# A trunk of token mixers on one core: inverse of both directions in lockstep, pair 0 prepared one stage earlier, gram products in four groups, two products per chunk in the recurrence

## What is computed

```python
def _rwkv_direction(r, w, k, v, a, b, s0):
    def step(state, inp):
        r_t, w_t, k_t, v_t, a_t, b_t = inp
        sa = jnp.einsum('bhvk,bhk->bhv', state, a_t)
        state = (state * w_t[:, :, None, :] + sa[..., None] * b_t[:, :, None, :]
                 + v_t[..., None] * k_t[:, :, None, :])
        return state, jnp.einsum('bhvk,bhk->bhv', state, r_t)
...
    kk = heads(k * lp['rw_k_k'])
    kk = kk * lax.rsqrt(jnp.maximum(jnp.sum(kk * kk, axis=-1, keepdims=True), 1e-24))
    k = k * (1.0 + (a - 1.0) * lp['rw_k_a'])
...
    a_vec, b_vec = -kk, kk * a
    o_f, s_f = _rwkv_direction(r, decay[:, :, 0], k, v, a_vec, b_vec, s0[:, 0])
    o_b, s_b = _rwkv_direction(_flip(r), _flip(decay[:, :, 1]), _flip(k), _flip(v),
                               _flip(a_vec), _flip(b_vec), s0[:, 1])
    o = o_f + _flip(o_b)
```

## Time and profile before

| | us |
|---|---|
| median of three runs (1967.83 to 1978.81) | 1972.71 |
| the profiled execution, its own time | 1975.78 |
| span of that execution | 1974.0 |
| PE busy | 1885.5 (96%) |
| DVE busy | 1092.9 (55%) |
| ACT busy | 744.2 (38%) |
| POOL busy | 32.1 (2%) |
| mixers stage, layer 0 (470.5 to 700.8) | 230.3 |
| mixers stage, layer 1 (1427.3 to 1649.1) | 221.8 |

### The profile page before, as it was taken

The page is one execution under the profiler, slowest core; times in us unless marked ns, Lnnn a source line. Parts: engine busy times, 40 slices in busy tenths (PEclk is TensorE's granted clock), DMA queues, the critical chain, the costliest instruction groups (busy, mean ns, idle before and its releaser), DMA issues. The chain is left out here.

```text
span 1974.0 us, 38649 instructions
## 1 busy us (share of the span) xinstructions
PE 1885.5 (96%) x16410; PEld 1739.0 (88%) x16410; DVE 1092.9 (55%) x1853; ACT 744.2 (38%) x1117; POOL 32.1 (2%) x64
## 2 busy tenths in 40 slices
PE   5999999998889999999999999999978899999998
PEld 3988999996666789999999999999947688999997
DVE  3544444865766475555455554477576746655533
ACT  3333333345334254333343333344363324433322
POOL 0000000000001000000000000000000100000000
PEclk9999999998999999999999999999989999999999
DMA  7766233423446343332343333342241412333332
GB/s 280 275 221 220 103 119 136 176 86 93 129 152 219 115 147 128 127 123 100 132 147 128 127 116 108 127 187 95 78 131 49 130 50 87 128 117 119 106 132 91
DMA packets 73335, 263.25 MB, mean 133 GB/s; under 512 B 9712, under 2 KB 11120, under 8 KB 57072
## 3 DMA queue, kind: packets, MB, share of 16 engines
q1 hardware_dynamic: 73200, 261.27, 39.0%
HBM read 259.08 MB, written 2.16 MB: 132 GB/s over the span
## 5 line engine op out<-in xcount | busy, mean ns | idle before, releaser
L160 PE MATMUL ps<-h_head,w_head 128*128 128x386 f32 x1824 | 623.5, 342 | 4.1 <-ACT h_head L293 2.1
L160 PE MATMUL ps<-h_head,w_rest 128*128 128x386 f32 x1824 | 619.3, 340 | 0.0
L160 PE MATMUL ps<-h_rest,w_head 128*128 128x386 f32 x1824 | 617.3, 339 | 0.0
L223 ACT ACTIVATE w_head<-w_raw 128x2048 fp32r<-128x2048 f32 (+1 forms) x176 | 303.0, 1722 | 606.0 <-PE ps L160 588.8
L226 DVE TENSOR_TENSOR w_rest<-w_raw,w_head 128x2048 fp32r<-128x2048 f32 (+1 forms) x176 | 360.6, 2049 | 209.3 <-ACT w_head L223 209.3
L160 PEld LDWEIGHTS ps<-h_head,w_head 128*128 128x128 f32 x1824 | 345.8, 190 | 23.1 <-issue 16.9
L160 PEld LDWEIGHTS ps<-h_head,w_rest 128*128 128x128 f32 x1824 | 345.9, 190 | 0.0
L160 PEld LDWEIGHTS ps<-h_rest,w_head 128*128 128x128 f32 x1824 | 343.0, 188 | 0.2
L160 PE MATMUL ps<-gu_head,w_head 128*128 128x384 f32 x832 | 278.4, 335 | 0.1
L160 PE MATMUL ps<-gu_head,w_rest 128*128 128x384 f32 x832 | 277.7, 334 | 0.0
L160 PE MATMUL ps<-gu_rest,w_head 128*128 128x384 f32 x832 | 277.7, 334 | 0.0
(11 more groups left out here) (300 smaller groups left out, 1784.2 us busy)
## 6 DMA issues: line engine op xcount, KB each, us to landing
w_raw<-in_w_in SPq DMA_DIRECT2D x88, 1024.0 KB, 4.8
w_raw<-in_w_out SPq DMA_DIRECT2D x64, 704.0 KB, 4.1
w_raw<-in_ada_w SPq DMA_DIRECT2D x41, 1024.0 KB, 6.3
ada_raw<-in_ada_w SPq DMA_DIRECT2D x31, 1024.0 KB, 6.3
w_raw<-in_mix_in SPq DMA_DIRECT2D x26, 1024.0 KB, 4.8
w_raw<-in_mix_out SPq DMA_DIRECT2D x8, 1024.0 KB, 5.0
hyena_const<-in_hconst SPq DMA_DIRECT2D x2, 1792.0 KB, 9.4
x<-in_x_in SPq DMA_DIRECT2D x1, 1536.0 KB, 12.1
```

Source lines behind the costliest of these rows:

```text
L160: return nc.tensor.matmul(out, lhsT, rhs, start=start, stop=stop)
L223: return nc.scalar.activation(self.HI[src], self.RAW[src], ACT.Copy)
```

## The change

Four parts, all in `mix_in_stage`, `mixers_stage` and `Pair`.

1. **Lockstep.** `each` goes through both directions inside each chunk and head, so that four products on the four 64x64 quadrants follow each other. Direction 1 reads or writes the other half of the partitions (`near`, `far`); its additions on DVE and GpSimd become two instructions of 64 partitions each.
2. **Gram.** Four groups (direction, three chunks) of 64x128 on two banks, and the turned keys as products of their own against a constant identity (`pe_turn_keys`), copied out by ACT from a third bank. The identity that GpSimd wrote is gone.
3. **Recurrence.** New `pe_values_in` (gram of the keys with the values), `pe_turn_a` and `pe_solve_a` (inverse with a), all ahead of the recurrence; its step is then `pe_y` and `pe_u`, without the copy to `XS`.
4. **Places.** Pair 0's low-rank products, norm, scans, exponentials and unit keys go into units n = 10 to 12 of `mix_in_stage`; pairs B and C are prepared together while A is in its recurrence (C with bank 6 alone); one `Ada` of two slots carries all sets. Each engine has a list for layer 0 (four sets) and another for layer 1 (two).

```diff
-            def each(self, b, lhsT, rhs):
-                for c, e in PROBS:
-                    last = mm(bank(b, TOK)[half(e), c * C:c * C + C], lhsT(c, e), rhs(c, e))
-                return last
+            def each(self, banks, lhsT, rhs, name, to):
+                for c in range(NCH):
+                    for e in range(2):
+                        for z in range(2):
+                            last = mm(bank(banks[z], TOK)[half(to[z] ^ e), c * C:c * C + C], lhsT(z, c, e), rhs(z, c, e))
...
+            def near(self, z, e):
+                return half(e)
+            def far(self, z, e):
+                return half(e ^ z)
...
-            def pe_s2(self, pe, z):
-                ba, _ = self.pair_banks(z)
-                self.after_act(pe, f"s1_{z}")
-                self.after_dve(pe, f"s1_{z}")
-                self.pe_step(self.each(ba, self.power(z), self.of(self.D2, z)), f"s2_{z}")
+            def pe_s2(self, pe):
+                self.both(pe, self.after_act, "s1")
+                self.both(pe, self.after_dve, "s1")
+                self.each(self.first_banks(), self.power(self.far), self.of(self.D2, self.far), "s2", (0, 0))
...
+            def side(self, z, first, second, name):
+                for c in range(NCH):
                     for e in range(2):
-                        at = (self.b0 + ((3 * z + b) * 2 + e) % 3) * 512 + k * 192
-                        last = mm(PS[:, at:at + 192], self.BK[half(e), z, 2 * b + k, :, :].rearrange("p x t -> p (x t)"),
-                                  self.AR[half(e), z, b, 2 * k:2 * k + 3, :].rearrange("p x t -> p (x t)"))
-                self.pe_step(last, f"gram{z}{b}")
+                        last = mm(bank(self.b1, TOK)[half(e), c * C:c * C + C], first(z, c, e), second(z, c, e))
+                self.pe_step(last, f"{name}_{z}")
...
+            def pe_turn_keys(self, pe, z, e):
...
+                    self.after_act(pe, f"bt{(2 * z + e - 1) // 2}{(2 * z + e - 1) % 2}")
+                for c in range(NCH):
+                    last = mm(bank(self.b2, TOK)[:, c * C:c * C + C], self.BK[half(e), z, c, :, :].rearrange("p x t -> p (x t)"),
+                              cst("istack", 0, None, 64 * e, 64 * e + 64))
...
+            def pe_solve_a(self, pe):
+                self.both(pe, self.after_dve, "s9")
+                self.both(pe, self.after_act, "at")
+                self.each(self.first_banks(), lambda z, c, e: self.MR[half(e), z, c, 1, 0:C], self.of(self.Y, self.near), "w", (0, 0))
...
             def dve_y(self, dve, i, z):
                 ba, _ = self.pair_banks(z)
                 self.after_pe(dve, f"s{i}_{z}")
-                self.tt(self.Y[:, z, :, :], self.XQ[:, z, :, 1, :], bank(ba, TOK).rearrange("p (c t) -> p c t", t=C), ALU.add, f"s{i}_{z}")
+                product = bank(ba, TOK).rearrange("p (c t) -> p c t", t=C)
+                if z == 0:
+                    last = nc.vector.tensor_tensor(self.Y[:, 0, :, :], self.XQ[:, 0, :, 1, :], product, ALU.add)
+                else:
+                    for e in range(2):
+                        last = nc.vector.tensor_tensor(self.Y[half(e), 1, :, :], self.QB[half(e)], product[half(1 - e)], ALU.add)
+                self.dve_step(last, f"s{i}_{z}")
...
+                        if n == 10:
+                            A.act_key_rate(act)
+                            A.act_key_factor(act)
+                            A.act_decays(act)
+                            A.act_key_root(act)
...
-                B.shared_free, C.shared_free = (A.act_done, A.AC["s6_1"]), (B.act_done, B.AC["s6_1"])
-                half = sets // 2
-                C_RAW = Place(B_AT.at)
-                ADAS = (Ada(None, SEMS[10:15], 2, [7] * half, 1, None, mod_row),
-                        Ada(C_RAW, SEMS[26:32], 3, [7] * half, 1, None, PR[:, 0:2 * NP - 2:NP, 0:ADA_W // 2].unsqueeze(1)))
+                B.shared_free, C.shared_free = (C.dve_done, C.DV["kk"]), (B.act_done, B.AC["s6_1"])
+                ADA = Ada(None, SEMS[10:15], 2, [7] * sets, 1, None, mod_row)
```

More of the change, by code:

```diff
@@ new lines, in each, with both @@
+            def each(self, banks, lhsT, rhs, name, to):
[3 more added lines that the diff above has]
+                            last = mm(bank(banks[z], TOK)[half(to[z] ^ e), c * C:c * C + C], lhsT(z, c, e), rhs(z, c, e))
+                            if name and (c, e) == (NCH - 1, 1):
+                                self.pe_step(last, f"{name}_{z}")
+            def both(self, pe, after, *names):
+                for name in names:
+                    for z in range(2):
+                        after(pe, f"{name}{z}" if name == "q" else f"{name}_{z}")
@@ L1738, in pe_spread_v @@
                 self.after_dve(pe, "vinv")
[L1739 to L1745 removed]
+                self.pe_step(spread_heads(self.b2, self.NRV), "vspread")
             def pool_decay(self, pool):
@@ L1940, in dve_power_q @@
                     nc.vector.tensor_copy(xq[:, :, :, 0, :], products[:, :, :, 0, :])
-                    last = nc.vector.tensor_tensor(xq[:, :, :, 1, :], xq[:, :, :, 1, :], products[:, :, :, 1, :], ALU.add)
+                    if z == 0:
+                        last = nc.vector.tensor_tensor(xq[:, :, :, 1, :], xq[:, :, :, 1, :], products[:, :, :, 1, :], ALU.add)
+                    else:
+                        q1 = self.QB[:, first:first + 3 * n, :].rearrange("p (b c) t -> p b c t", b=n)
+                        for e in range(2):
+                            last = nc.vector.tensor_tensor(q1[half(e)], xq[half(1 - e), :, :, 1, :], products[half(e), :, :, 1, :], ALU.add)
                 self.dve_step(last, f"s2q_{z}")
@@ L1946, in dve_q @@
                 self.after_pe(dve, f"s{i}_{z}")
-                self.tt(self.XQ[:, z, :, 1, :], self.XQ[:, z, :, 1, :], bank(bb, TOK).rearrange("p (c t) -> p c t", t=C), ALU.add, f"s{i}_{z}")
+                product = bank(bb, TOK).rearrange("p (c t) -> p c t", t=C)
+                if z == 0:
+                    last = nc.vector.tensor_tensor(self.XQ[:, 0, :, 1, :], self.XQ[:, 0, :, 1, :], product, ALU.add)
+                else:
+                    old, new = (self.QB, self.XQ[:, 1, :, 1, :]) if i == "3q" else (self.XQ[:, 1, :, 1, :], self.QB)
+                    for e in range(2):
+                        last = nc.vector.tensor_tensor(new[half(e)], old[half(1 - e)], product[half(e)], ALU.add)
+                self.dve_step(last, f"s{i}_{z}")
             def dve_y(self, dve, i, z):
@@ new lines, in mixers_stage @@
+                assert homes.ceiling <= nc.sbuf_top and LEFT.at <= homes.early_at and RIGHT.at <= late_at
+                B_ROWS, B_LEFT, B_RIGHT = Place(homes.rows_at), Place(homes.above), Place(homes.right_at)
+                B = Pair(Place(0, gram=B_ROWS, bonus=B_ROWS, ar_identity=B_LEFT, bk=B_LEFT, bk_tok=B_LEFT, uv=B_LEFT, state_t=B_LEFT, chunk_decay=B_LEFT, power4=B_LEFT,
+                               power_and_q=B_RIGHT, sig_w=B_RIGHT, cum=B_RIGHT, decay_incl=B_RIGHT, decay_inv=B_RIGHT),
+                         SEMS[15:20], lay, 1, (3, 4, 5), 6, PR, TG, AL, MO)
```

1933 lines of the change are left out of this document (1247 added, 686 removed).

## The result

The changed kernel takes 1997.45 us (median of 4 runs, 1985.85 to 2013.17) beside 1970.27 us of the kernel before on the same chip: ratio 1.0139, interval 1.0096 to 1.0181. It is **slower by some 27 us**; 1944 was forecast, with 1908 to 1968 as the range. The profiled execution took 1999.16 us with a span of 1997.4.

What follows compares the result with a forecast made beforehand. It took TensorE, busy 96% of the span, as the bound. Per stage -20 (PE's work) - 11 (start) + 14 (new waits) = -17, twice -34; `mix_in_stage` twice +2.7: -29, so 1944 us, range 1908 to 1968.

Steps and rivals of the forecast that it cites:

- The inverse: In the mixers stages' inverse, four quadrants at once were to take 16 ns a record, saving 8.2 us per pair.
- 25 ns floor: Rival: an inverse record takes 25 ns instead of 16, so the kernel takes 1964 us; chance 0.08.
- no gain: Rival: four quadrants don't run at once, an inverse level stays at 1.40 us, giving 1981 us; chance 0.05.
- New side products: `pe_values_in`, `pe_turn_a` and `pe_solve_a`, ahead of the recurrence, were to add 3.8 us per pair.
- Gram: Gram and turned-key groups in the mixers stages: between +0.9 and +6.9 us per pair, taken as +1.0.
- Recurrence: Two product groups per recurrence step instead of three were to save 2.3 us per pair.
- The start: Earlier first products at each mixers stage's start, less idle time and slow clock: -11 us; `mix_in_stage` +2.7 each.
- New waits of the lockstep chain: PE waiting for DVE between inverse levels, 5 us per pair out of 0 to 13: +14 us per stage.
- the other work covers it: Rival: other products fill the gaps between inverse levels, the +14 falls to nearly nothing, giving 1916 us; chance 0.20.
- Loads: One `Ada` with two slots on SP does the mixers stages' loads of two and three slots, costed at nothing.
- a mean of 0.90, +20 us: Rival: more gaps lower the granted clock over the whole stage to a mean of 0.90, giving 1964 us; chance 0.10.

Runs made afterwards that it cites:

- thin loads: The changed kernel with each `ada` weight load in the mixers cut to a quarter of its bytes, products unchanged: 1974.83 us, ratio 1.0009 to the kernel before.

## Why the prediction was wrong

The forecast was 1944. Without the clock's loss the change is 6 us faster than before, with it 25 slower, by the medians of this table. Two steps failed most: the sum kept the stages' clock at 0.96 and 0.94, where it was 0.88 and 0.91 (30 us over the run), and it had no term for the instructions' arrival (20.7 us more of `issue` in the two stages). Step by step, first the steps that give PE's work:

- **The inverse: right.** 16 ns a record were taken, 15 to 18 measured; the rivals of the 25 ns floor and of "no gain" are out. Two quadrants did run at once before, and four do now. But the 57 ns for one alone came from the wrong row: 342 ns is a record's length, not the time to the next (such records start 176 ns apart, as at 473.34 and 473.51 above), and these are split products with one record each (114 loads of 1 MB with 16 blocks make the 1824), not two, as I had written of every product. The right rows of the kernel before are those of plain products on the full array:

```profile
394.72 5.34 PE L160 MATMUL ps<-mixer_out,hyena_const 128*128 128x256 f32 x24
399.71 0.53 PE L160 MATMUL ps<-h_head,w_head 128*128 128x386 f32 x1
```

That is 208 ns for 256 columns, 52 ns for 64. So the 57 was near by luck, and the reading from it held: 29 ns a record on two quadrants is half of one alone. By the rule that I named (the Trainium skill, "TensorE: Matmul & The Clock Gate", section "Wait — 56ns, not 53.3ns?") 48 records would take 1.2 us, an estimate from its 25 ns; the row at 647.82 has 0.72. The other rule (the Trainium skill, "TensorEngine Tiling (Array Packing)", Gotcha 1) doesn't fit either: the two row halves write into one bank at 29 ns a record, and at 15 to 18 ns each of the two banks still takes both. In the sum a pair was to save 8.2 us; undoing it cost 18.0 and 14.5 per stage, 4.8 to 6 a pair.
- **New side products: too low.** I put `pe_solve_a` on four quadrants. Its own call (`near` on both sides, target `(0, 0)`) gives both directions the same two, and it took 1.6 us a group for 0.97; with the others some +4.8 a pair for +3.8.
- **Gram: the lower bound was the wrong choice.** The gram group took 0.77, as reckoned (0.81), the turned keys 1.38 instead of 0.7, nearer to the middle of my bounds: +3.5 a pair for +1.0. "The loads have been under the products elsewhere" was a mean over the run used for a shape that the trace of before didn't show: 12 records that all use one half of the rows and 128 columns of the array. Their weight loads take 188 ns (median), the upper bound; 115 a record lies between.
- **Recurrence: right in PE's time** (1.08 us for 1.09), wrong in worth. With its side products the sum made it a loss of 9 us (3.8 - 2.3 for six pairs), for the sake of one copy less in each step; undoing it cost 20 us.
- **The start: near in total** (11 to 17 us for 17), wrong in its path: I took the slow clock of the first 28 us as something that more work would cure. With the start full of work the clock there was 0.69 in stage 1, lower than 0.76, and each group took double, 1.55 us at 487.32, so 13.4 us instead of 8 to 10. In stage 2 it did rise, from 0.88 to 0.94 in the first 28 us. `mix_in_stage` grew by 3.4 and 3.6, over my "not more than 3".
- **New waits of the lockstep chain: wrong sign.** +14 a stage were forecast; waits other than `issue` and DMA fell by 7.1 and 5.6, and those on the levels' own evictions come to 2.4 and 5.2 us in all. The products between the levels cover DVE. That rival (1916, "the other work covers it") was right in mechanism, and its time was missed all the same.
- **Loads: nearly nothing**, as costed: waits on them rose from 1.0 and 0.5 us to 2.6 and 1.4. But by the thin loads their bytes hold up the instructions.
- **Instruction supply: not foreseen**, +14.1 and +6.6 us. The 5.4 us of `issue` in stage 1 stood in the trace of before and I hadn't asked where they fell. Halving a record's time halves the time that 256 instructions last, so this wait had to be costed with the very term that promised most.
- **The clock: the step that failed most.** The sum kept the stages' clock at 0.96 and 0.94. The rival "a mean of 0.90, +20 us" had a chance of 0.10 and was the main truth: 0.88 and 0.91, +30 us over the run. I put its cause in gaps alone. The runs show edits under which the loss shrinks: those that take waits away (thin loads -8, start in place -8 to -11, short recurrence -22), the inverse on two quadrants (-5 to -18, with 9 to 15 us more of other time), and keys on the full array (-19, with time without the clock unchanged and idle time in the stages not less: 34.0 and 37.4 us beside 33.8 and 31.6). Halving the loads, which only changed one wait for another, didn't lower it (60.8; with full-array keys 48.6 beside 38.6).

My own conditions for being wrong read `mix_in_stage` over 3 us, keys at 2 us, waits of 30 us a stage. The first came true by a little; neither of the two that mattered, clock and supply, was among them.

What stays open: the parts don't add up. Undoing the quadrants and the start singly moves the time by -4 and about +16, putting keys on the full array by -17, and undoing the recurrence on top of that by +20. The rest must lie in what wasn't tried alone, the gram groups with their masks in eight pieces on DVE and the order of the work as a whole, and in how the parts act on each other through the clock. Why the half level lasts longer with the half-array keys is not shown either, only that it does in these two kernels: the full-array groups are also shorter and have half the records. None of these kernels that brings all its bytes beats the kernel before; full-array keys come nearest, 0.4% above it.

## What to carry to other kernels

Reckon PE's time as work at full clock, loss by the clock, and waits, each from the records, before costing a change that trades many short products for few: a saving of work is worth its microseconds only while the clock holds and the instructions arrive. A group's price comes from start to start of a group with the same tile shape and place in the array; for a shape that the trace doesn't have, take the middle of the bounds. Read from the code which quadrants each product really uses. And where the trace shows small waits that no engine releases, look at which instruction number they fall on, because a faster group makes them grow first.

## What the hardware did that I had not expected

- PE stands still at one place in 256 of its own instructions when they run out: up to 4.21 us, resuming 2.2 to 2.9 us after the 16 KB packet's start. With a quarter of the load bytes the standstills of stage 1 were 4.6 us, for 19.5 and 13.1 in two executions with all of them.
- Plain records of 64x64 by 64 columns start 29 ns apart on two quadrants that write into one bank and 15 to 18 ns on four with neighbours in different banks; alone, by the 208 ns of the 256-column record, they would take 52 (an estimate).
- Records of 64 columns start 115 ns apart where all use the same row half and 128 columns of the array (turned keys), twice that estimate; their weight loads take 188 ns. On the full array, with 128 columns, it is 145 ns (0.87 us for 6).
- In two kernels that do the same work, the half level of the clock cost 57.9 us with the turned keys on one row half and 38.6 with them on the full array.
